# Memory loaded in four parts a group sooner, and three small moves beside it, in a one-core decoder layer

## What is computed

```
h = x + 0.5 * swiglu(norm(x) @ w_ffn1_in) @ w_ffn1_out
B, C, H, U, V = split(norm(h) @ w_mix_in)
y_conv = B * causal_dwconv3(C * H)
y_gm   = U * (tril(w_spatial[head]) @ norm(V) + b_spatial)
h = h + concat(y_conv, y_gm) @ w_mix_out
q, k, v = norm(h) @ w_xq, norm(mem) @ w_xk, norm(mem) @ w_xv
h = h + (softmax(q k^T / sqrt(512)) v) @ w_xo
h = h + 0.5 * swiglu(norm(h) @ w_ffn2_in) @ w_ffn2_out
out = norm(h) * g_final
```

## Time and profile before

| | |
|---|---|
| median of 3 runs | 2136.78 us |
| the profiled execution's own time | 2138.68 us |
| its span, first to last instruction | 2136.9 us |
| PE busy | 2124.8 us (99%) |
| DVE / ACT / POOL busy | 1462.7 / 964.2 / 92.9 us |
| chain that ended last, by engine | PE 95%, DVE 3%, DMA 1% |
| data read from HBM | 409.01 MB, 192 GB/s over the span |
| granted TensorE clock | 0.999 of full speed |

### The profile page before, as it was taken

How to read it: one execution, slowest core, us unless ns; L and a number is a source line. 1 busy time by engine, 2 the same in 40 slices (tenths; PEclk the granted TensorE clock), 3 DMA queues, 4 the chain that set the end, 5 groups by cost and what they waited for, 6 DMA issues and landing times.

```text
span 2136.9 us, 23530 instructions
## 1 busy us (share of the span) xinstructions
PE 2124.8 (99%) x9480; PEld 1763.7 (83%) x9480; DVE 1462.7 (68%) x1754; ACT 964.2 (45%) x1090; POOL 92.9 (4%) x43
## 2 busy tenths in 40 slices
PE   9999999999999999999999999999999999999998
PEld 7888888888888888888888888888888888888887
DVE  6776667666465587879898884687676667664544
ACT  6444444444344444444554444445444444443433
POOL 2000000000000000014300320000000000000000
PEclk9999999999999999999999999999999999999999
DMA  8666666665555666665555555566666666655554
GB/s 266 192 193 197 190 195 196 190 195 197 192 192 195 191 195 194 192 222 188 192 194 195 171 172 172 173 210 195 191 195 193 192 195 192 193 195 194 192 195 149
DMA packets 159825, 412.65 MB, mean 193 GB/s; under 512 B 12652, under 2 KB 14308, under 8 KB 159332
## 3 DMA queue, kind: packets, MB, share of 16 engines
q1 hardware_dynamic: 158160, 409.78, 62.2%
q10 hardware_dynamic: 1556, 1.37, 0.2%
HBM read 409.01 MB, written 2.10 MB: 192 GB/s over the span
## 4 chain that ended last, share of the span: by engine, by line
PE 95%; DVE 3%; DMA 1%; ACT 0%; issue 0%; ACTq 0%; DVEq 0%
PE ps L1180 94%; PE ps L1207 1%; DVE ps L745 1%; DVE w_lo L685 1%; DMA mem_nat<-in_mem 0%; DVE ps L1062 0%; PE ps L1265 0%; PE ps L1343 0%; DMA rows<-in_g_ffn 0%; PE ps L1230 0%; DVE memT_nat L756 0%; PE ps L1259 0%; DVE xT_lo L701 0%; DVE stage L848 0%; DVE stage L964 0%
## 5 line engine op out<-in xcount | busy, mean ns | idle before, releaser
L685 DVE TENSOR_TENSOR w_lo<-raw,w_hi 128x1024 fp32r<-128x1024 f32 x732 | 911.5, 1254 | 561.3 <-ACT w_hi L365 554.5
L365 ACT ACTIVATE w_hi<-raw 128x1024 fp32r<-128x1024 f32 x767 | 805.8, 1061 | 968.9 <-PE ps L1180 954.0
L1180 PE MATMUL ps<-w_hi,xT_hi 128*128 128x512 f32 x1848 | 494.5, 389 | 1.0 <-ACT w_hi L365 1.0
L1180 PE MATMUL ps<-w_lo,xT_hi 128*128 128x512 f32 x1848 | 493.9, 389 | 0.0
L1180 PE MATMUL ps<-w_hi,xT_lo 128*128 128x512 f32 x1848 | 493.9, 389 | 0.0
L1180 PEld LDWEIGHTS ps<-w_hi,xT_hi 128*128 128x128 f32 x1848 | 346.6, 188 | 73.3 <-DVE xT_lo L693 1.4
L1180 PEld LDWEIGHTS ps<-w_hi,xT_lo 128*128 128x128 f32 x1848 | 346.9, 188 | 72.0
L1180 PEld LDWEIGHTS ps<-w_lo,xT_hi 128*128 128x128 f32 x1848 | 346.9, 188 | 71.9
L745 DVE STREAM_TRANSPOSE ps<-stage 32x256 f32<-32x256 f32 (+1 forms) x464 | 241.4, 520 | 8.5
L1180 PE MATMUL ps<-w_hi,hidT_lo 128*128 128x512 f32 x700 | 188.5, 389 | 0.0
L1180 PE MATMUL ps<-w_lo,hidT_hi 128*128 128x512 f32 x700 | 188.5, 389 | 0.0
(11 more groups left out here) (143 smaller groups left out, 910.5 us busy)
## 6 DMA issues: line engine op xcount, KB each, us to landing
raw<-in_w_ffn_in SPq DMA_DIRECT2D x351, 512.0 KB, 4.6
raw<-in_w_ffn_out SPq DMA_DIRECT2D x176, 512.0 KB, 4.5
raw<-in_w_mix_in SPq DMA_DIRECT2D x80, 512.0 KB, 4.4
raw<-in_w_mix_out SPq DMA_DIRECT2D x32, 512.0 KB, 4.5
raw<-in_w_xq SPq DMA_DIRECT2D x32, 512.0 KB, 4.4
raw<-in_w_xk SPq DMA_DIRECT2D x32, 512.0 KB, 4.5
raw<-in_w_xv SPq DMA_DIRECT2D x32, 512.0 KB, 3.8
raw<-in_w_xo SPq DMA_DIRECT2D x32, 512.0 KB, 4.2
```

The lines of the kernel that those rows point to most:

```text
L365: nc.scalar.activation(w_hi[:, u % RING, :], raw[:, u % RAW, :], ACT.Copy).then_inc(hi_ready, 1)
L685: nc.vector.tensor_tensor(w_lo[:, u % RAW, :], raw[:, u % RAW, :], w_hi[:, u % RING, :].bitcast(F32), ALU.subtract).then_inc(lo_ready, 1)
L1180: ins = nc.tensor.matmul(bank(s, t * GW + b * BLK, BLK), xs[:, k, t * P:(t + 1) * P], ws_[:, (unit0 + k) % (RING if ws_ is w_hi else RAW), ...
```

## The change

Seven things, of which the first four belong together:

1. `wsT` moves into the 4 KB of `scratch`, so the memory's place is free as soon as the FFN's hidden values are.
2. The memory is loaded in four parts of 512 KB (token tile by column half), each after four unit loads of group V, with no wait of its own.
3. DVE turns the first half of the memory whole inside U (units 9 to 15), and the second half in mix_out0 (8 instructions) and mix_out1 (8). Nothing is left for q0.
4. POOL no longer makes `w_lo` of units 1 and 3 of mix_out0; DVE does.
5. In k1 and v0 POOL takes units 5, 7, 8, 10, 12, 14 (was 5, 7, 9, 11, 13, 15), and DVE starts to turn k one unit earlier.
6. x tiles 0 and 1 are loaded one by one; PE turns tile 0, and tile 1 only after four passes of unit 0; `warm(4)` becomes `warm(1)`; tiles 2 and 3 are turned one pass earlier in unit 1. ACT rounds unit 2 before it scales tiles 2 and 3.
7. At the end the third gain product goes from DVE to POOL.

```diff
-X_PARTS = ((0, 2), (2, 4), (4, 8), (8, 12), (12, 16))
+X_PARTS = ((0, 1), (1, 2), (2, 4), (4, 8), (8, 12), (12, 16))
...
-    pool_units = [*range(UNIT0["ffn1_in0"] + 7, UNIT0["ffn1_in0"] + 15, 2),
-                  *range(UNIT0["mix_out0"] + 1, done("mix_out1"), 2), *range(UNIT0["q0"] + 5, UNIT0["q0"] + 13, 2),
-                  *range(UNIT0["k1"] + 5, done("k1"), 2), *range(UNIT0["v0"] + 5, done("v0"), 2)]
+    pool_units = [*range(UNIT0["ffn1_in0"] + 7, UNIT0["ffn1_in0"] + 15, 2), *range(UNIT0["mix_out0"] + 5, done("mix_out0"), 2),
+                  *range(UNIT0["mix_out1"] + 1, done("mix_out1"), 2), *range(UNIT0["q0"] + 5, UNIT0["q0"] + 13, 2),
+                  *(UNIT0[name] + k for name in ("k1", "v0") for k in (5, 7, 8, 10, 12, 14))]
...
+    at_scratch = place["at"]
     scratch = put("scratch", [P, GW], F32)
+    wsT = put("wsT", [P, HEADS, P], F32, at=at_scratch)
...
-    wsT = put("wsT", [P, HEADS, P], F32, at=big + 64 * KB)
...
             load_x(0)
             sp.dma_start(raw[:, 0, 0:BLK], first(0)[:, 0, :]).then_inc(half_loaded, 16)
             sp.dma_start(raw[:, 0, BLK:GW], first(0)[:, 1, :]).then_inc(raw_loaded[0], 16)
+            load_x(1)
             load_units(first, 0, 2, 1)
-            load_x(1)
+            load_x(2)
...
-            for name, c in (("C", 1), ("H", 2), ("B", 0), ("V", 4), ("U", 3)):
+            for name, c in (("C", 1), ("H", 2), ("B", 0)):
                 load_units(cols_src(w_mix_in, c * GW), UNIT0[name], KD)
-
-            sp.wait_ge(gated, 4)
-            sp.dma_start(mem_nat[:, :, :], mem[0].rearrange("(t p) n -> p t n", p=P)).then_inc(mem_loaded, 16)
+            for n in range(4):
+                load_units(cols_src(w_mix_in, 4 * GW), UNIT0["V"], 4 * n + 4, 4 * n)
+                t, c = n % 2, n // 2
+                sp.dma_start(mem_nat[:, t, c * GW:(c + 1) * GW], mem[0, t * P:(t + 1) * P, c * GW:(c + 1) * GW]
+                             ).then_inc(mem_loaded, 16)
+            load_units(cols_src(w_mix_in, 3 * GW), UNIT0["U"], KD)
...
+            pool.wait_ge(staged, STAGED["ffn2_out1"] + 3)
+            nc.gpsimd.tensor_tensor(stage[:, 1, 0:BLK], h[:, 1, GW:GW + BLK], g_fin[:, GW:GW + BLK],
+                                    ALU.mult).then_inc(gained_pool, 1)
...
+            act.wait_ge(turned, TURN["x0"] + 1)
             nc.scalar.activation(xT_hi[:, 1, :], bank(1, 7 * SEQ, SEQ), ACT.Copy, scale=col("g_ffn1", 1)).then_inc(hi_taken, 1)
-            hi_units(0, 1, 2)
+            hi_units(0, 1, 3)
             hi_scaled(xT_hi, 0, "g_ffn1", 1, "x0", 1, 2)
-            hi_units(0, 2, 3)
...
-            act.wait_ge(gained, TOK + 3)
+            act.wait_ge(gained_pool, 1)
...
-            lo_units(u, 8, 15)
-            dve.wait_ge(mem_loaded, 16)
-            turn_mem(0, u, 15, 0, 1)
-            turn_sbuf(memT_nat[:, 0:HALF, :], mem_nat[:, :, 0:GW], mem_turned, 2, 4)
+            lo_units(u, 8, 9)
+            dve.wait_ge(mem_loaded, 16 * 4)
+            turn_mem(0, u, 9, 0, 7)
+            turn_sbuf(memT_nat[:, 0:HALF, :], mem_nat[:, :, 0:GW], mem_turned, 14, 16)
...
-            turn_mem(0, u, 11, 2, 7)
-            turn_sbuf(memT_nat[:, 0:HALF, :], mem_nat[:, :, 0:GW], mem_turned, 14, 16)
+            turn_mem(1, u, 11, 0, 4)
+            lo_units(u, 15, KD)
...
-                if i < 5:
-                    turn_sbuf(memT_nat[:, HALF:KD, :], mem_nat[:, :, GW:D], mem_turned, 2 * i, 2 * i + 2)
+                if i % 2 == 0:
+                    turn_sbuf(memT_nat[:, HALF:KD, :], mem_nat[:, :, GW:D], mem_turned, 8 + i, 10 + i)
...
-            turn_mem(1, u, 13, 5, 8)
+            lo_units(u, 13, KD)
...
-            end_gain(2)
             end_rstd(1, 4, 2)
```

More of the change, by code:

```diff
@@ L217, in build @@
         first_half = sem("first_half")
+        tile_turned = sem("tile_turned")
         tile_hi = sem("tile_hi")
@@ L253, in build @@
         gained = sem("gained")
+        gained_pool = sem("gained_pool")
         out_ready = [sem(f"out_ready{c}") for c in range(2)]
@@ L301, in _ @@
             sp.dma_start(raw[:, 0, BLK:GW], first(0)[:, 1, :]).then_inc(raw_loaded[0], 16)
+            load_x(1)
             load_units(first, 0, 2, 1)
-            load_x(1)
+            load_x(2)
             load_units(first, 0, 3, 2)
-            load_x(2)
+            load_x(3)
             load_units(first, 0, 4, 3)
-            load_x(3)
             load_x(4)
+            load_x(5)
             load_ffn_in(1, w_ffn1_in, 4)
             load_pair("ffn1_out", w_ffn1_out, KF)
-            for name, c in (("C", 1), ("H", 2), ("B", 0), ("V", 4), ("U", 3)):
+            for name, c in (("C", 1), ("H", 2), ("B", 0)):
                 load_units(cols_src(w_mix_in, c * GW), UNIT0[name], KD)
-            sp.wait_ge(gated, 4)
-            sp.dma_start(mem_nat[:, :, :], mem[0].rearrange("(t p) n -> p t n", p=P)).then_inc(mem_loaded, 16)
+            for n in range(4):
[4 more added lines that the diff above has]
+            load_units(cols_src(w_mix_in, 3 * GW), UNIT0["U"], KD)
             load_pair("mix_out", w_mix_out, KD)
@@ L455, in _ @@
             act.wait_ge(cols_ready, 1)
-            act.wait_ge(turned, TURN["x0"] + 1)
+            act.wait_ge(tile_turned, 1)
             nc.scalar.activation(xT_hi[:, 0, :], bank(1, 0, SEQ), ACT.Copy, scale=col("g_ffn1", 0)).then_inc(tile_hi, 1)
@@ L871, in _ @@
             lo_units(0, 6, 7)
-            dve.wait_ge(x_loaded[4], 16)
+            dve.wait_ge(x_loaded[5], 16)
             dve.wait_ge(turned, TURN["x1"] + 2)
@@ L1038, in _ @@
                 scaled(name, rstd_mem)
-                lo_units(u, 3, 5)
+                lo_units(u, 3, 4)
                 dve.wait_ge(staged, STAGED[name] + TOK)
@@ L1042, in _ @@
                     turn_blocks(stage[:, :, :], SET[name], HALF, 4 * i, 4 * i + 4)
-                    lo_units(u, 5 + i, 6 + i)
+                    lo_units(u, 4 + i, 5 + i)
                 lo_plain(kT_lo, kT_hi, pair * HALF, SET[name], 2, HI[name])
                 lo_plain(kT_lo, kT_hi, pair * HALF + 4, SET[name], 2, HI[name] + 2, b0=2)
-                lo_units(u, 9, 13)
+                lo_units(u, 8, 13)
                 dve.wait_ge(scored, pair + 1)
@@ L1274, in _, with turn_first @@
             nc.tensor.transpose(bank(0, 0, KD), rows[0:KD, :], ident[0:KD, 0:KD]).then_inc(rows_turned, 1)
-            warm(4)
-            pe.wait_ge(x_loaded[0], 16)
-            for k, at in ((0, 0), (1, 7 * SEQ)):
+            warm(1)
+            def turn_first(k, at):
+                pe.wait_ge(x_loaded[k], 16)
                 for t in range(TOK):
                     ins = nc.tensor.transpose(bank(1, at + t * P, P), h[:, t, k * P:(k + 1) * P], ident[:, :])
-            ins.then_inc(turned, 1)
+                return ins
+            turn_first(0, 0).then_inc(tile_turned, 1)
             warm(8)
@@ L1289, in _ @@
             first_pass(0, xT_lo, w_hi, (1,))
+            turn_first(1, 7 * SEQ).then_inc(turned, 1)
             pe.wait_ge(lo_ready, 1)
@@ L1294, in _ @@
             first_pass(1, xT_hi, w_hi, (0, 1))
+            pe.wait_ge(x_loaded[2], 16)
+            turn(from_half(h, 0), 1, X_PARTS[2][1], X_PARTS[2][0])
             pe.wait_ge(taken, TAKEN["x0"] + 1)
             first_pass(1, xT_lo, w_hi, (0, 1))
-            pe.wait_ge(x_loaded[1], 16)
-            turn(from_half(h, 0), 1, X_PARTS[1][1], X_PARTS[1][0])
             pe.wait_ge(lo_ready, 2)
@@ L1302, in _ @@
             group("ffn1_in0", xT_hi, xT_lo, 2, 3)
-            pe.wait_ge(x_loaded[2], 16)
-            turn(from_half(h, 0), 1, X_PARTS[2][1], X_PARTS[2][0])
+            pe.wait_ge(x_loaded[3], 16)
+            turn(from_half(h, 0), 1, X_PARTS[3][1], X_PARTS[3][0])
             group("ffn1_in0", xT_hi, xT_lo, 3, 4)
@@ L1307, in _ @@
             group("ffn1_in0", xT_hi, xT_lo, 4, 5)
-            pe.wait_ge(x_loaded[3], 16)
+            pe.wait_ge(x_loaded[4], 16)
             pe.wait_ge(taken, TAKEN["x0"] + 4)
```

## The result

Medians of 20 runs each on one chip: 2141.44 us after, 2137.41 us before. The ratio is 1.0018, with a 95% interval of 1.0012 to 1.0025: the change makes the kernel **4.0 us slower**, 0.18%. Carried to the 2136.78 us shown of before, the forecast of -1.25 us was out by over 5 us, and the value lies outside the range given. Of the 20 runs of after, 19 lie in two heaps (the twentieth is an outlier of 12 ms): eight from 2140.2 to 2140.9 us, six of which show a mean granted clock of 0.999, and eleven from 2141.4 to 2142.0, all at 0.998. The profiled one, 2141.62 us for a span of 2139.9, is of the second heap. The profiled execution of before, 2138.68 us, is longer than all but two of the 118 other runs of before on record (one outlier of 3.6 ms left out), so the two traces lie closer together than the medians do.

What follows compares the result with a forecast made beforehand. PE bounds the kernel, busy 2124.8 of 2136.9 us, so scheduling can win only 12.1 us. The terms -0.5 - 1.5 - 0.25 + 1.0 = -1.25 us take the median from 2136.78 to 2135.5 us, range 2134.1 to 2137.3.

Steps and rivals of the forecast that it cites:

- the last of k1 and v0: Scores behind k1 and v0: `xT_lo` ready some 3 us sooner, covering DVE's extra `w_lo` of 1.2 us; gain 0.25 us.
- mix_out0, -1.5: U and mix_out0: gate's product 2.5 us sooner, `yT_lo` at 972.2, PE no longer waits; gain 1.5 us, low end 0.7.
- The start, -0.5: Start: first pass at 6.25, unit 2 at about 14.45 instead of 15.01; gain 0.5 us, between nothing and 1.1.
- the slow spell: Unit 0's slow first matmuls: the first eight end at about 9.0 if it goes by wall clock, else 8.7.
- The forecast wait at unit 1: Start: ACT scales tile 1 before rounding unit 1, so PE gets a new wait of 0.7 us for its `w_hi`.
- The end, +1.0: End: POOL's product holds `end_part` and everything behind it 1.07 us, less 0.1 gained; 1.0 us lost.
- rival A: End costs nothing, as `end_part` has one column: sum -2.35 us, 2134.4 us; chance 0.2.
- B: Slower than before, POOL's last product ahead of `end_part` outweighs the gains: 2137.1 to 2137.8 us; chance 0.15.
- D: More than 4.3 us faster, against which stands too little idle time in the places touched; chance 0.01.
- C: Wait moves: DVE falls behind in U or loads stall behind the memory's parts; 2140 us and more; chance 0.03.
- The 0.97 for "within 0.2%": Whole kernel: chance 0.97 that the time stays within 0.2% (4.3 us) of before; 0.01 faster, 0.02 slower.

Runs made afterwards that it cites:

- the two clean pairs: Two pairs of changed kernels differing only in whether POOL or DVE makes the third gain product, in one set and at one clock: 0.57 and 0.72 us.

## Why the prediction was wrong

**The step that failed** is the last of k1 and v0: "DVE has one `w_lo` more behind the scores, 1.2 us, which the 3 us cover". I took the turns' earlier place as a gain of DVE's time and set the 1.2 us against it, with POOL left out: "POOL off DVE's path". In v0 it was the other way round: these 1.2 us bring DVE behind POOL's unit 5 instead of ahead of it, and then each of DVE's next three `w_lo`, of units 3, 4 and 6, starts inside one of POOL's, the third because POOL's new list has unit 10. Instead of a gain, PE stood 2.91 us for unit 6. What was needed was the same walk through the timeline that the prediction made for mix_out0, row by row, with POOL's starts set by ACT's. All durations for it were in the earlier trace rows: 1.22, 5.87, 2.40. Forecast -0.25, measured +4.9. The forecast's own view of this place had only DVE's last operation in it, and no row of POOL.

**A term that the sum did not have** is the clock. I counted a wait as what it lasts; here 2.9 us of standing brought another 1.4 and 1.6 us behind it in two of three profiles.

**mix_out0, -1.5.** The mechanism was right in every step (3.32 us forecast as 3.3, product 2.5 us sooner, no wait), and 1.54 is the difference of the two traces. (The 2.72 us in its sum are a whole unit's twelve matmuls, not three quarters of one; the sum is right.) As a term of the median it was mis-sized: of four traces with the old memory only that of before has the wait, and the part alone measures -0.24. The prediction had a sign of it: it noted that the profiled execution was 1.9 us over the median, and took a wait from that execution as if every one had it.

**The start, -0.5.** Mis-sized too, in the trace: 1.08. The first pass came at 5.53, not 6.25, as the wait of 0.7 us for the gain vector went too, which the sum did not have (it is in all four traces with the old start and in none of the ten with the new). The first eight matmuls took some 2.1 us, until tile 1's turn at 7.62, where I had them end at 8.7 to 9.0; in other traces with the new start they took up to 2.8, so whether the slow spell goes by count or by time is not settled. The forecast wait at unit 1 is there, 1.37 instead of 0.7, and 0.58 of it is the landing of the weights and not ACT's queue. The turn of tiles 2 and 3 ended at 11.88 and not 12.56, so unit 2 began at 13.93, not 14.45, though DVE's half of the tiles ended 2.0 us behind it and not 1.8. In the median, though, the part alone measures -0.15.

**The end, +1.0.** Right in kind, against rival A: 0.88 at `end_part`, some 0.1 back in the tail, 0.6 to 0.7 us by the two clean pairs. The 1.0 was somewhat too large. One detail was wrong. I had POOL behind the scaling, until 2129.5. POOL began 0.16 us behind the scaling's start, the scaling kept its 0.74 us, and POOL took 1.74 for 512 columns. The Trainium skill, "GPSIMD Engine Reference", section 1, would have both in the way; for `end_part` the trace agrees, with 1.05 against 0.16 us. For the scaling it shows no delay on DVE's side, and POOL's time is 0.5 us above half of its 2.40; whether POOL stood for the scaling no run here separates.

**The rivals.** The result is none of A, B and D. It is nearest to C, "the wait moves: DVE falls behind", in kind and in size, but in v0, not in U. C had a chance of 0.03, as I had looked for it only in the place where the change moves most instructions. The 0.97 for "within 0.2%" are right by the median, 0.18%, though the interval of the ratio reaches 0.25%; that it came out so is no merit of the mechanism.

## What to carry to other kernels

In these traces the time of a DVE or POOL step depends on which of the two arrives first. One short operation more, far ahead of the place, together with one changed unit in POOL's list, turned a schedule in which POOL works beside DVE's turns into one where each of DVE's `w_lo` stands for POOL. So walk both engines' timelines through every place where either's list of work changes, and count a wait of PE with what the clock may do behind it. If a wait is seen in one trace, above all in one whose time is over the median, look for it in another before its removal is counted as a gain.

## What the runs showed of the hardware

- The granted clock was at 1.00 through PE's stand of 2.9 us and averaged 0.52 and 0.63 in the 4 us behind it; in an execution of another kernel with the same stand it stayed 1.00. With matmuls of zeros in the stand it stayed 1.00 too.
- An operation of one column with both inputs in SBUF stood 0.89 us beside POOL: 1.05 instead of 0.16.
- The port is held both ways. POOL's `w_lo` of 2.40 us took 2.73 to 3.47 where DVE's was already waiting or running. The Trainium skill, "SBUF — State Buffer", section "🔬 SBUF: two separate sides", says that whichever of the two starts first gets the pair of ports for its whole instruction and the other fully blocks. By these rows the trace agrees, and so the order of arrival is what decides.
